# One operation for both heads in the attentions, row sums added up on VectorE, and stick-breaking attention in pairs of heads

## What is computed

```python
# first block: two layers of attention and a squared-ReLU MLP, both with modulation from c
u = modulate(rms_norm(h, g), shift, scale)
# layer 0: neighbourhood attention of 256 queries over 512 keys with a bias table,
#          and context attention of 256 queries over 256 keys
# layer 1: sliding-window attention of 256 queries over 512 keys, with a sink
p = jax.nn.softmax(s, axis=-1)
h = h + gate * (attention @ w_o);  h = h + gate2 * (square(relu(u @ w1)) @ w2)
# second block: S5 state-space mixer with a gated output, gated MLP, stick-breaking attention, gated MLP
z = einsum('bqhd,bkhd->bhqk', q, k) * scale
log_beta = log_sigmoid(z)
log_1m = where(causal, log_beta - z, 0.0)
later = cumsum(log_1m, axis=3, reverse=True) - log_1m
w = where(causal, exp(log_beta + later), 0.0)
```

## Time and profile before

| | us |
|---|---|
| median of three runs (lowest, highest) | 1920.46 (1920.42, 1923.15) |
| profiled execution, its own time | 1921.01 |
| its span from first to last instruction | 1919.1 |
| PE busy in the span | 1730.0 |
| DVE busy | 1179.3 |
| ACT busy | 882.4 |
| POOL busy | 96.5 |

### The profile page before, as it was taken

The page is one execution under the profiler, slowest core; times in us unless marked ns, Lnnn a source line. Parts: engine busy times, 40 slices in busy tenths (PEclk is TensorE's granted clock), DMA queues, the critical chain, the costliest instruction groups (busy, mean ns, idle before and its releaser), DMA issues.

```text
span 1919.1 us, 36849 instructions
## 1 busy us (share of the span) xinstructions
PE 1730.0 (90%) x13240; PEld 1503.3 (78%) x13240; DVE 1179.3 (61%) x2051; ACT 882.4 (46%) x1587; POOL 96.5 (5%) x152
## 2 busy tenths in 40 slices
PE   4899999899999989698889998788999887879999
PEld 3678766687888767574689998688999886569999
DVE  5674594543224445668667776756775566757774
ACT  4564484343223323454554544245554465435553
POOL 0000120000000012100000203100000000000000
PEclk8999999899999999897999998899999988999999
DMA  9444442253344355320145656633555333025554
GB/s 358 147 179 178 159 122 80 97 187 143 135 161 174 140 181 172 114 102 1 45 167 202 199 196 222 254 132 116 191 177 195 132 132 110 0 88 167 183 191 149
DMA packets 79686, 291.48 MB, mean 152 GB/s; under 512 B 10000, under 2 KB 11792, under 8 KB 77408
## 3 DMA queue, kind: packets, MB, share of 16 engines
q1 hardware_dynamic: 69120, 248.96, 37.0%
q0 software_dynamic: 10464, 41.15, 6.6%
HBM read 271.39 MB, written 18.68 MB: 151 GB/s over the span
## 4 chain that ended last, share of the span: by engine, by line
PE 76%; DVE 13%; ACT 6%; issue 3%; DMA 1%; POOL 0%; DVEq 0%; ACTq 0%; SPq 0%; POOLq 0%
PE bank L601 21%; PE bank L602 20%; PE bank L603 20%; PE bank L511 2%; DVE stat L1752 2%; PE bank L661 1%; PE bank L662 1%; PE bank L663 1%; PE bank L780 1%; PE bank L791 1%; PE bank L680 1%; PE bank L673 1%; DVE w_lo L1364 1%; PE bank L804 1%; ACT w_hi L997 1%
## 5 line engine op out<-in xcount | busy, mean ns | idle before, releaser
L601 PE MATMUL bank<-u_hi,w_hi 128*128 128x256 f32 (+1 forms) x1936 | 622.6, 322 | 67.5 <-DVE u_lo L1571 34.6
L1364 DVE TENSOR_TENSOR w_lo<-raw,w_hi 128x1024 fp32r<-128x1024 f32 x372 | 454.2, 1223 | 268.0 <-ACT w_hi L997 251.7
L602 PE MATMUL bank<-u_lo,w_hi 128*128 128x256 f32 (+1 forms) x1936 | 607.6, 314 | 0.0
L603 PE MATMUL bank<-u_hi,w_lo 128*128 128x256 f32 (+1 forms) x1936 | 607.2, 314 | 0.0
L997 ACT ACTIVATE w_hi<-raw 128x1024 fp32r<-128x1024 f32 x360 | 377.7, 1050 | 239.0 <-PE bank L603 215.1
L601 PEld LDWEIGHTS bank<-u_hi,w_hi 128*128 128x128 f32 x1936 | 380.2, 196 | 98.4 <-issue 73.4
L602 PEld LDWEIGHTS bank<-u_lo,w_hi 128*128 128x128 f32 x1936 | 380.1, 196 | 21.0 <-issue 2.9
L603 PEld LDWEIGHTS bank<-u_hi,w_lo 128*128 128x128 f32 x1936 | 379.3, 196 | 18.9
L601 PE MATMUL bank<-hid_hi,w_hi 128*128 128x512 f32 (+1 forms) x512 | 178.9, 349 | 5.7 <-ACT hid_hi L1043 5.7
L602 PE MATMUL bank<-hid_lo,w_hi 128*128 128x512 f32 (+1 forms) x512 | 173.6, 339 | 0.0
L603 PE MATMUL bank<-hid_hi,w_lo 128*128 128x512 f32 (+1 forms) x512 | 173.4, 339 | 0.0
(11 more groups left out here) (294 smaller groups left out, 2448.8 us busy)
## 6 DMA issues: line engine op xcount, KB each, us to landing
raw<-weights SPq DMA_DIRECT2D x372, 512.0 KB, 3.4
ada_raw<-ada_w SPq DMA_DIRECT2D x80, 512.0 KB, 6.0
ada_first<-ada_w SPq DMA_DIRECT2D x16, 512.0 KB, 15.4
bias_sb<-bias_na POOLq DMA_DIRECT2D x16, 256.0 KB, 3.2
toep_dram<-zeros POOLq DMA_DIRECT2D x8, 512.0 KB, 8.9
bat_dram<-bat POOLq DMA_DIRECT2D x16, 256.0 KB, 3.3
ca_dram<-ca POOLq DMA_DIRECT2D x16, 256.0 KB, 4.6
...
```

Source lines behind the costliest of these rows:

```text
L601: pe.matmul(dst, wh, hi[:, kt, xs], start=first, stop=False)
L602: pe.matmul(dst, wh, lo[:, kt, xs], start=False, stop=False)
L603: return pe.matmul(dst, wl, hi[:, kt, xs], start=False, stop=final)
L1364: TT(w_lo[:, slot, :], raw[:, slot, :], w_hi[:, slot, :].bitcast(F32), ALU.subtract).then_inc(S["lo"], 1)
```

## The change

- **Attentions.** PSUM is taken as four pairs of banks. Bias or window addition, maximum and the copy of the transposed weights are done in one operation for both heads. The exponentials (one per head, for their sums) and the scaling stay as they are.
- **Row sums.** VectorE adds the squares of each tile to `ssum` (`add_row`), TensorE multiplies by ones once at the end of the stage (`row_total`), and the norm reads that bank. In `glu` ScalarE squares each tile right after it is done, instead of all of them after the stage.
- **Stick-breaking.** Eight pairs of heads instead of sixteen heads, each operation 768 columns wide. The causal mask is put into the bank by a product of the identity with the mask (fp32r) ahead of the scores, so that both mask operations of VectorE are gone and the exponential reads the bank. The scores of pair p wait for the weights of pair p-3 (`sb_weights`). Sums come two steps after the scores, values three.
- **Preamble.** `bbar` is computed in two halves in `rotations(0)` and `rotations(11)`; the piece of `rotations(10)` is now `rotations(12)`.

```diff
-            c.update(a1=n, sq=n, d3=n // 4)
+            c.update(a1=n, d3=n, sq=1)
...
-                if s.kind == "QK":
-                    pe.wait_ge(S["a1"], value("a1", s, j + 1))
-                    pe.wait_ge(S["a2"], value("a2", s, j - 1))
-                    pe.matmul(SUM_BANKS[(s.tile0 + jj) % 2][:, 0:s.tok], C("block"), sq[:, (s.tile0 + jj) % 2, 0:s.tok],
-                              start=True, stop=True).then_inc(S["p2"], 1)
-                else:
-                    pe.wait_ge(S["a1"], value("a1", s, i * body + (jj + 1)))
-                    if jj == 0:
-                        pe.wait_ge(S["d3"], value("d3", s, i * 1))
-                    pe.matmul(SS[:, 0:s.tok], C("ones"), sq[:, jj % 2, 0:s.tok], start=(jj == 0),
-                              stop=(jj == body - 1)).then_inc(S["sq"], 1)
+                pe.wait_ge(S["a1"], value("a1", s, j + 1))
+                pe.wait_ge(S["a2"], value("a2", s, j - 1))
+                pe.matmul(SUM_BANKS[(s.tile0 + jj) % 2][:, 0:s.tok], C("block"), sq[:, (s.tile0 + jj) % 2, 0:s.tok],
+                          start=True, stop=True).then_inc(S["p2"], 1)
+            def row_total(name):
+                s = ST[name]
+                stage_end(pe, s, ("d3",))
+                pe.matmul(SS[:, 0:s.tok], C("ones"), ssum[:, 0:s.tok], start=True, stop=True).then_inc(S["sq"], 1)
...
-                sums = s.kind == "QK" or row_sums(s)
+                sums = s.kind == "QK"
...
-            drained("wo0")
+            row_total("wo0"); drained("wo0")
...
-            for kt in range(KT):
-                pe.wait_ge(S["a3"], value("a3", ST["glu"], kt + 1))
-                pe.matmul(SS[:, 0:SEQ], C("ones"), sq[:, kt % 2, 0:SEQ], start=(kt == 0), stop=(kt == KT - 1)).then_inc(S["sq"], 1)
+            row_total("glu")
...
+            def sb_scores(p):
+                if p >= 3:
+                    pe.wait_ge(sb_a2, p - 2)
+                for a in range(2):
+                    pe.matmul(bank_pair[p % 3][:, a, 0:384], ident_r[:, :], mask_r[:, :], start=True, stop=False,
+                              skip_group_check=True)
+                for keys, cols, qs in ((slice(0, P), slice(0, SEQ), slice(0, SEQ)), (slice(P, SEQ), slice(SEQ, 384), slice(P, SEQ))):
+                    for a in range(2):
+                        hs = slice(a * HD, (a + 1) * HD)
+                        mm = pe.matmul(bank_pair[p % 3][:, a, cols], k2[hs, p, keys], q2[hs, p, qs], start=False, stop=False,
+                                       skip_group_check=True)
+                mm.then_inc(sb_s, 1)
+            def sb_sums(p):
+                pe.wait_ge(sb_d2, p + 1)
+                for a in range(2):
+                    pe.matmul(bank_pair[p % 3][:, a, 0:384], C("ntri"), sb_r[:, p % 3, a, :], start=False, stop=False,
+                              skip_group_check=True)
+                for a in range(2):
+                    mm = pe.matmul(bank_pair[p % 3][:, a, P:SEQ], C("nones"), sb_r[:, p % 3, a, SEQ:384], start=False, stop=True,
+                                   skip_group_check=True)
+                mm.then_inc(sb_c, 1)
+            def sb_values(p):
+                pe.wait_ge(sb_a2, p + 1)
+                if p >= 2:
+                    pe.wait_ge(sb_l, p - 1)
+                for t, cols, ws in ((0, slice(0, SEQ), slice(0, SEQ)), (1, slice(P, SEQ), slice(SEQ, 384))):
+                    for a in range(2):
+                        n = 2 * p + a
+                        mm = pe.matmul(psum[6 + p % 2][a * HD:(a + 1) * HD, cols], val2[:, t, n * HD:(n + 1) * HD],
+                                       sb_w[:, p % 2, a, ws], start=(t == 0), stop=(t == 1), skip_group_check=True)
+                mm.then_inc(sb_o, 1)
+            pe.wait_ge(sb_m, 1)
+            for n in range(KT + 3):
+                if n < KT:
                     sb_scores(n)
-                if 1 <= n <= HEADS:
-                    sb_sums(n - 1)
-                if 2 <= n:
-                    sb_values(n - 2)
+                if 0 <= n - 2 < KT:
+                    sb_sums(n - 2)
+                if 0 <= n - 3 < KT:
+                    sb_values(n - 3)
...
-                        act.wait_ge(S["sq"], value("sq", s, j - 1))
+                        act.wait_ge(S["d3"], value("d3", s, j - 1))
...
+                    act.wait_ge(S["d1"], value("d1", s, pair + 1))
+                    act.wait_ge(S["d3"], value("d3", s, pair - 1))
+                    A(sq[:, pb, 0:SEQ], h[:, bass.ds(pair, 1), 0:SEQ].rearrange("p a t -> p (a t)"),
+                      ACT.Square).then_inc(S["a3"], 1)
...
-                for a in range(2):
-                    act.wait_ge(att_t, 2 * g + a + 1)
-                    if g >= 2:
-                        act.wait_ge(att_o, g - 1)
-                    A(prob_t[:, 2 * (g % 2) + a, 0:keys], psum[4 + a][:, 0:keys], ACT.Copy).then_inc(att_e, 1)
+                act.wait_ge(att_t, 2 * g + 2)
+                if g >= 2:
+                    act.wait_ge(att_o, g - 1)
+                gs = slice(2 * (g % 2), 2 * (g % 2) + 2)
+                A(prob_t[:, gs, 0:keys], bank_pair[2][:, :, 0:keys], ACT.Copy).then_inc(att_e, 2)
...
+            A(mask_r[:, :], C("causal_neg"), ACT.Copy)
+            A(ident_r[:, :], C("ident"), ACT.Copy).then_inc(sb_m, 1)
...
+            for n in range(KT + 4):
+                p = n
+                if p < KT:
+                    act.wait_ge(sb_d1, p + 1)
+                    if p >= 2:
+                        act.wait_ge(sb_d2, p - 1)
+                    chain.link(A(sb_e[:, p % 2], sb_n[:, p % 2], ACT.Exp))
+                    A(sb_e[:, p % 2], sb_e[:, p % 2], ACT.Ln, bias=C("ones")[:, 0:1]).then_inc(sb_a1, 1)
+                p = n - 2
+                if 0 <= p < KT:
+                    act.wait_ge(sb_c, p + 1)
+                    if p >= 2:
+                        act.wait_ge(sb_o, p - 1)
+                    A(sb_w[:, p % 2], bank_pair[p % 3][:, :, 0:384], ACT.Exp).then_inc(sb_a2, 1)
...
+                    if row_sums(s) and jj:
+                        add_row(s, "a1", j - 1, jj - 1)
...
+            def add_row(s, squared, j, b):
+                dve.wait_ge(S[squared], value(squared, s, j + 1))
+                dve.wait_ge(S["d3"], value("d3", s, j))
+                TT(ssum[:, 0:s.tok], ssum[:, 0:s.tok], sq[:, b % 2, 0:s.tok], ALU.add).then_inc(S["d3"], 1)
...
-                        dve.wait_ge(S["sq"], value("sq", s, i * 4 + 4))
-                        link(TT(ssum[:, 0:s.tok], SS[:, 0:s.tok], ssum[:, 0:s.tok], ALU.add))
-                        dve.nop().then_inc(S["d3"], 1)
+                        add_row(s, "a1", i * body + body - 1, body - 1)
...
+            def bbar_part(im):
+                d, t = bbar[:, im], rot0[:, 2, :, 0:SSM_H]
+                link(TT(d, b_in[:, 0], (v(23), v(16))[im].unsqueeze(2).to_broadcast([P, PAIRS, SSM_H]), ALU.mult))
+                link(TT(t, b_in[:, 1], (v(16), v(23))[im].unsqueeze(2).to_broadcast([P, PAIRS, SSM_H]), ALU.mult))
+                link(TT(d, d, t, (ALU.subtract, ALU.add)[im]))
...
+                if u == 0:
+                    dve.wait_ge(b_in_in, 16)
+                    bbar_part(0)
+                elif u == 11:
+                    bbar_part(1)
+                    dve.nop().then_inc(pre_v, 1)
...
-                s_ = [psum[2 * (g % 2) + a] for a in range(2)]
-                for a in range(2):
-                    dve.wait_ge(att_s, 2 * g + a + 1)
-                    if kind == "na":
-                        if a == 0:
-                            dve.wait_ge(bias_in[b], 16 * (g // 4 + 1))
-                        add = TT(s_[a][:, 0:SEQ], s_[a][:, 0:SEQ], bias_sb[:, b, a, :], ALU.add)
-                    elif kind == "swa":
-                        cut = slice((1 - qt) * P, (2 - qt) * P)
-                        add = TT(s_[a][:, cut], s_[a][:, cut], C("window")[:, qt * P:(qt + 1) * P], ALU.add)
-                    if kind != "ctx":
-                        link(add)
-                for a in range(2):
-                    red = dve.tensor_reduce(stat[:, 0, b, a:a + 1], s_[a][:, 0:keys], AX.X, ALU.max, negate=True)
-                    if kind == "swa":
-                        link(red)
-                    else:
-                        red.then_inc(att_m, 1)
+                both = bank_pair[g % 2]
+                dve.wait_ge(att_s, 2 * g + 2)
+                if kind == "na":
+                    dve.wait_ge(bias_in[b], 16 * (g // 4 + 1))
+                    link(TT(both[:, :, 0:SEQ], both[:, :, 0:SEQ], bias_sb[:, b, :, :], ALU.add))
+                elif kind == "swa":
+                    cut = slice((1 - qt) * P, (2 - qt) * P)
+                    window = C("window")[:, qt * P:(qt + 1) * P].unsqueeze(1).to_broadcast([P, 2, P])
+                    link(TT(both[:, :, cut], both[:, :, cut], window, ALU.add))
+                red = dve.tensor_reduce(stat[:, 0, b, :], both[:, :, 0:keys], AX.X, ALU.max, negate=True)
...
-            for n in range(HEADS + 2):
```

(40 more changed lines are left out.)

111 lines of the change are left out of this document (35 added, 76 removed).

## The result

The changed kernel takes 1866.23 us (median of 4 runs, 1862.82 to 1869.23), the kernel before 1920.6 (median of 4, 1920.42 to 1923.15). The ratio is 0.9713, with a 95% interval of 0.9695 to 0.9732: 54 us less, where 50.6 were forecast. Run again later, the same kernel took 1864.12 us against 1920.29.

What follows compares the result with a forecast made beforehand. TensorE was busy 1730.0 of 1919.1 us; gains were sought in its removable work and waits, stage by stage. Terms 2.4 + 5.5 + 13.5 + 23.1 + 2 + 2.6 + 1.5 = 50.6 from 1921.01: forecast 1870, range 1859 to 1885.

Steps and rivals of the forecast that it cites:

- 2.4 and 5.5 were forecast: Attentions: merging operations of both heads gains 2.4 us in ATT0's bias groups and 5.5 us in ATT1.
- rule of a fixed latency per operation: Attentions: each merge saves some 150 cycles, .16 us; ATT1 then gains about 1 us less, bias groups unchanged.
- The term was 13.5: Stick-breaking: pairs of heads shorten the stage from 65.7 to 52 us, at 6.1 us a pair, gaining 13.5 us.
- I take the first 17 us at that level: Stick-breaking: TensorE's clock stays at 1.2 GHz for the first 17 us; scores of pair 3 end at 15.9 us.
- The 2 us put on top for sums ahead of scores: Stick-breaking: one pair's sums (2.1 us) can stand once ahead of the next scores, so 52 us instead of 50.0.
- The rival in which the clock stays low: Stick-breaking: clock stays at .50 throughout, a pair takes 8.5 us, the stage 69, the kernel 1887 us; chance 10%.
- Mask operations removed from VectorE are most of what makes the loop shorter: Stick-breaking: removing mask operations (2 of 5 per head) from VectorE is most of the loop's shortening; no separate size.
- 23.1 were forecast: Row sums, six stages: moving sums of squares off TensorE gains 13 + 3.8 + 2.5 + 3.8 = 23.1 us.
- The 2 for the stage ends: Ends of down0b and down1b: ScalarE's copies of table_kernel stand ahead of less, about 1 us each, 2 in all.
- At the stage's end ... nothing: Row sums, stage ends: last sum waits .45 us for an addition but needs one product fewer; no net change.
- The term was 2.6: End of glu: eight sums of 4.93 us become square, addition, one product and hand-overs, gaining 2.6 us.
- 1.5 as forecast: Preamble: the first w_lo no longer waits behind bbar and starts at about 37.5, gaining 1.5 us.

Runs made afterwards that it cites:

- pairs_vector_mask: Changed kernel with stick-breaking's mask kept on VectorE, no identity product, and scores waiting for VectorE's exponent instead of ScalarE's weights: 1865.01 us.
- weights_first: Changed kernel with ScalarE's stick-breaking weights of pair p-2 ahead of exp and log of pair p instead of behind them: 1857.71 us.
- h_first: Changed kernel with VectorE's addition to h ahead of the tile's last lower half, in all stages with row sums: 1875.04 us.
- both_orders: Changed kernel with ScalarE's weights of pair p-2 ahead of exp and log of p, and addition to h first in wo1 and wo2 alone: 1851.12 us.

## Why the prediction was right, and where it was not

**Attentions.** 2.4 and 5.5 were forecast, 2.2 and 5.4 came. Some .6 of the 5.4 is the clock: from the start of ATT1 it was low for 9 us in this profile and for 12 in that of before, and in the eight further profiles of the new attention in which it was low for 11 to 12 us the stage took 61.5 to 61.9 us. So the merges gave 4.6 to 4.9 of the 5.5. The merged addition takes .69 where two took .89, the maxima 1.22 where two took 1.42 with a wait each, as read from the rows. I had weighed the Trainium skill's rule of a fixed latency per operation ("VectorE: DVE Perf Modes", The TRN2 errata) at .16 a merge. The Trainium skill states it for operands in SBUF; here the scores lie in PSUM. Measured, a merge saves .20 where the second operation waited for the first, as both additions and the reductions of ATT1 did, and .07 where it did not and the two overlapped (1.29 to 1.22 from start to end, the reductions of ATT0). The rule's .16 lies between the two; the wait decides.

**Stick-breaking.** The mechanism and the pace were right, 6.06 for 6.1 a pair; among the links the mask took .55 for .36, and mask and scores together 1.52 for 1.46. The term was 13.5 and measured 14.9, with errors on both sides. "I take the first 17 us at that level" failed: with three pairs' scores and masks in a row TensorE was never idle at the start and its clock was up 7.7 us after it; the scores of pair 3 ended at 13.9 us, not 15.9 (the terms there add up to 15.8). The 2 us put on top for sums ahead of scores did not come, since those sums lie in TensorE's waits. On the other hand the clock fell twice later: one turn took 7.01 instead of 6.06, and the sums from 1623.50 took 2.68 instead of 1.56, so that the tail was 11.2 instead of 9.7. That these nearly cancel is luck. The rival in which the clock stays low did not come, though it was not absent: windows at .73 and .57 are small pieces of it. The Trainium skill ("TensorE: Matmul & The Clock Gate", HAM oscillation) has waits between bursts pull the clock down. Here that is seen from 1608.7 and from 1622.4, behind waits of 1.86 us, and not behind another as long (1602.44).

The step "Mask operations removed from VectorE are most of what makes the loop shorter" was wrong. With them back the stage took 49.35 us. I had listed the loop's links rightly and then not asked which of them each edit touched: VectorE's mask operations were hardly in that loop. `pairs_vector_mask` changes two things, the place of the mask and the gate of the scores; that the gate on ScalarE's weights gave away what the mask product took from VectorE is the reading that fits it and `weights_first`, and no kernel has the one without the other.

**Row sums.** 23.1 were forecast and 24.2 measured over the six stages; undoing them, with `glu`, cost 29.1, against my 27.7 for sums, stage ends and `glu`. The 2 for the stage ends came as 1.1 and 1.3, from the norm's first step to the next product: ScalarE's eight copies of `kern` (1.75 us) stood ahead of the norm's first logarithm before, so that TensorE waited 10.89 and 5.73 us for `u_lo`, and now stand ahead of nothing, 9.39 and 4.42. `wo1` and `wo2` gave 1.2 and 1.6 of 1.9 each. The ScalarE and VectorE loop of the earlier trace rows stays, as forecast; in `wo2` the step between the bodies, 5.00 before, became 3.44 and not 3.16. "At the stage's end ... nothing" did not hold for these two: TensorE's products now end 4.2 and 4.0 us earlier in the stage, but it waits for the loop behind them: from the last product to the norm it was 3.32 and 2.75 us and is 6.34 and 5.10. `h_first` and `both_orders` show that the loop is the order of `w_lo` and the addition, not the engines' work. The stretch with `down0b` gave 1.3 more than its terms; that stays open.

**glu.** The term was 2.6, and the stretch was to be under 2 us. From the last product (1304.7 before, 1271.4 after) to the norm's first step it was 5.8 and is 4.0, so 1.8 was won: the steps for the last pair (sigmoid, product, addition, square, addition) stand in a row, while the sums of before had begun during them. The row of 4.93 us was not the path's length. The rest of that stretch (2.6) is the norm's 1.3 just told, and differences that go both ways: the input product took 25.8 and 24.6, the mixer 42.8 and 45.2, `glu` itself 52.4 and 49.8, with a clock of .61 around 1260 before and .91 at that place now. I put them down to the clock, which no run separates from the rest.

**Preamble.** From the first upper half to the first product it was 8.90 us and is 7.42, 1.5 as forecast; it is the same in all twelve profiles with the new preamble. The stretch as a whole says less: it took 213.80 to 217.61 us in these twelve, against the 217.46 of before, because the first upper half starts anywhere from 35.07 to 36.89 (36.38 before) and by the clock. So 2.2 of its 3.7 us, and as much of the total's 55, belong to this one profile.

The total was close (1866.2 for 1870) because nearly every term came from a loop or a stall that could be read off the trace. The errors were of 1 to 2 us each, mostly on the clock, and they partly cancelled.
